# The final output stage in pairs of token tiles: seven block products per pair in place of eight

## What is computed

```python
y = _branch_out(hm.astype(x.dtype), g, w_out)      # (o * silu(g)) @ w_out, 1024 x 1024
return x + gate * y, sf, sb
...
y_sample = _rmsnorm(x, final_norm_w)               # and the same for y_prompt
```

## Time and profile before

| what | value |
|---|---|
| median of the runs | 2621.69 us |
| the profiled execution's own time | 2623.37 us |
| its span, first to last instruction | 2621.6 us |
| TensorE busy | 2573.6 us, 98% of the span |
| VectorE, ScalarE, GpSimd busy | 46%, 34%, 24% |
| mean granted TensorE clock | 0.995 of full speed |

### The profile page before, as it was taken

One profiled execution on the slowest core, in us unless ns is written; L12 is line 12 of the kernel. 1 busy time (PEld: TensorE's weight loads), 2 busy tenths in 40 slices (PEclk: granted clock), 3 DMA queues, 4 the chain that ended last, 5 costly groups with the idle time before them and its releaser, 6 DMA issues.

```text
span 2621.6 us, 49672 instructions
## 1 busy us (share of the span) xinstructions
PE 2573.6 (98%) x18563; PEld 2247.6 (86%) x18563; DVE 1199.6 (46%) x3271; ACT 895.3 (34%) x2118; POOL 623.4 (24%) x816
## 2 busy tenths in 40 slices
PE   6999999999999999999999999999999999999998
PEld 3788888888888887887999999999999999999786
DVE  5664646646465566553242333414242332515433
ACT  5463635626354473223122221313122131314111
POOL 1412232131222213331031120404022130403332
PEclk8999999999999999999999999999999999999999
DMA  9702122030221225431041221304132121316543
GB/s 358 258 23 70 50 58 71 18 98 14 67 64 45 71 63 178 136 122 58 23 75 48 46 85 27 96 17 87 44 59 64 39 85 19 85 44 171 162 146 107
DMA packets 188733, 219.63 MB, mean 84 GB/s; under 512 B 27248, under 2 KB 133504, under 8 KB 186576
## 3 DMA queue, kind: packets, MB, share of 16 engines
q1 hardware_dynamic: 181888, 195.93, 26.8%
q10 hardware_dynamic: 6608, 20.55, 2.0%
HBM read 178.27 MB, written 38.17 MB: 83 GB/s over the span
## 4 chain that ended last, share of the span: by engine, by line
PE 59%; DVE 2%; issue 1%; POOL 0%; ACT 0%; DVEq 0%; POOLq 0%
PE psum L560 12%; PE psum L562 12%; PE psum L561 12%; PE psum L2559 2%; PE psum L2084 2%; PE psum L2626 2%; PE psum L2085 2%; PE psum L2086 2%; PE psum L1611 2%; PE psum L1613 2%; PE psum L1612 2%; PE psum L2629 2%; PE psum L2607 1%; PE psum L2550 1%; PE psum L2514 1%
## 5 line engine op out<-in xcount | busy, mean ns | idle before, releaser
L560 PE MATMUL psum<-h_hi,m_w_lo 128*128 128x384 f32 (+1 forms) x1600 | 594.0, 371 | 0.0
L562 PE MATMUL psum<-h_hi,m_w_hi 128*128 128x384 f32 (+1 forms) x1600 | 573.6, 358 | 0.0
L561 PE MATMUL psum<-h_lo,m_w_hi 128*128 128x384 f32 (+1 forms) x1600 | 573.1, 358 | 0.0
L562 PEld LDWEIGHTS psum<-h_hi,m_w_hi 128*128 128x128 f32 x1600 | 300.5, 188 | 27.0
L560 PEld LDWEIGHTS psum<-h_hi,m_w_lo 128*128 128x128 f32 x1600 | 301.3, 188 | 24.5 <-issue 1.6
L561 PEld LDWEIGHTS psum<-h_lo,m_w_hi 128*128 128x128 f32 x1600 | 301.6, 189 | 22.4
L560 PE MATMUL psum<-h_hi,attn_w_lo 128*128 128x384 f32 (+1 forms) x800 | 294.1, 368 | 0.6 <-DVE attn_w_lo L545 0.6
L562 PE MATMUL psum<-h_hi,attn_w_hi 128*128 128x384 f32 (+1 forms) x800 | 285.9, 357 | 0.0
L561 PE MATMUL psum<-h_lo,attn_w_hi 128*128 128x384 f32 (+1 forms) x800 | 285.5, 357 | 0.0
L1049 DVE CUSTOM_DVE_ANT_0 arena<-psum,wmask,stats 128x640 f32<-128x640 f32 (+2 forms) x256 | 206.0, 839 | 74.5 <-PE psum L1269 73.7
L963 ACT ACTIVATE arena<-arena,stats 128x640 f32<-128x640 f32 (+2 forms) x272 | 213.5, 786 | 70.9 <-DVE stats L1049 69.9
(11 more groups left out here) (343 smaller groups left out, 4629.4 us busy)
## 6 DMA issues: line engine op xcount, KB each, us to landing
m_bc<-gate_rows_mlstm SPq DMA_DIRECT2D x124, 256.0 KB, 3.4
m_w_raw<-in_mlstm_w_in SPq DMA_DIRECT2D x40, 512.0 KB, 4.8
h_full<-gated_output SPq DMA_DIRECT2D x29, 512.0 KB, 4.2
gated_output<-gT SPq DMA_DIRECT2D x8, 1088.0 KB, 5.2
layer_output<-xb_out ACTq DMA_DIRECT2D x17, 512.0 KB, 2.6
h_hi_full<-layer_output SPq DMA_DIRECT2D x17, 512.0 KB, 4.9
out<-h_hi_full ACTq DMA_DIRECT2D x17, 512.0 KB, 5.2
attn_w_raw<-in_attn_w_in SPq DMA_DIRECT2D x16, 512.0 KB, 6.5
```

The source lines that it names most:

```text
L560: pe.matmul(out, self.lo[:, k, :], E.h_hi[:, k, tok], start=(k == 0), stop=False)
L561: pe.matmul(out, self.hi[:, k, :], E.h_lo[:, k, tok], start=False, stop=False)
L562: ins = pe.matmul(out, self.hi[:, k, :], E.h_hi[:, k, tok], start=False, stop=(k == KT - 1))
```

## The change

Tiles 0 to 4 stay as they are. Tiles 5 to 16 are taken as six pairs q = 0 to 5, with tiles b = 5 + 2q and a = 6 + 2q. A pair is regarded as a 2 x 2 block matrix: two tiles of tokens by two halves of the contraction. The output weights are a 2 x 2 block matrix too: two halves of the contraction by two halves of the columns. The eight block products of the ordinary scheme become seven products of sums of blocks, each of 12 matmuls of 128x512. What it adds:

- SP: at the head of `sp_late`, four loads of 1 MB with blocks of the output weights and the two 512 KB loads of pair 0; only behind them the `og` load of tile 3. Pairs 1 to 5 are loaded as pairs.
- VectorE: four combinations of weight blocks, 2048 columns wide (`combined`), behind `og_low(3)` and ahead of the gate multiplication of tile 1; four low parts of the same width behind tiles 1 and 2 (`combined_low`); per pair four low parts (`pair_low`, one of 512 and three of 1024 columns), five additions of 512 columns out of PSUM, and two gate multiplications that now read SBUF.
- ScalarE: four high parts of 2048 columns, behind the square of tile 0 and ahead of the square of tile 1; per pair four high parts and two copies out of PSUM (`p1`, `c11`).
- GpSimd: per pair four additions or subtractions of 512 columns per partition (`pair_sums`) in place of two casts.
- TensorE: waits between the seven products of a pair, since three PSUM banks are accumulated into, read in between, and accumulated into again.

Unchanged parts of the helpers, and their allocation, are left out of this cut of the diff:

```diff
+    FIRST = 5
+    PAIRS = (NT - FIRST) // 2
+    ROWS2, ROWS1, S12, S34 = range(4)
...
+    def sp_blocks(self, sp):
+        w_out = self.E.a["mlstm_w_out"][0].rearrange("(k p) m -> p k m", p=P)
+        for i, (k0, c0) in enumerate(((0, 0), (0, 512), (4, 512), (4, 0))):
+            sp.dma_start(self.t_raw[i], w_out[:, k0:k0 + 4, c0:c0 + 512]).then_inc(self.s_tx, 16)
...
+    def pair_sums(self, pool, q):
+        two, one, s12, s34 = self.pair_raw[q % 2]
+        first, second = slice(0, 4), slice(4, 8)
+        a11, a12, a21, a22 = one[:, first, :], one[:, second, :], two[:, first, :], two[:, second, :]
+        s1, s2, s3, s4 = s12[:, first, :], s12[:, second, :], s34[:, first, :], s34[:, second, :]
+        pool.wait_ge(self.s_pair[q % 2], 32 * (q // 2 + 1))
+        if q < 2:
+            pool.wait_ge(self.s_y, (3, self.FIRST)[q])
+        settle(self.E, pool)
+        pool.tensor_tensor(s1, a21, a22, ALU.add).then_inc(self.s_S, 1)
+        pool.tensor_tensor(s3, a11, a21, ALU.subtract).then_inc(self.s_S, 1)
+        pool.wait_ge(self.s_S, 4 * q + 1)
+        pool.tensor_tensor(s2, s1, a11, ALU.subtract).then_inc(self.s_S, 1)
+        pool.wait_ge(self.s_S, 4 * q + 3)
+        pool.tensor_tensor(s4, a12, s2, ALU.subtract).then_inc(self.s_S, 1)
...
+    ORDER = (1, 0, 2, 3)
+
+    def pair_high(self, act, q):
+        act.wait_ge(self.s_pair[q % 2], 32 * (q // 2 + 1))
+        if q == 1:
+            act.wait_ge(self.s_y, self.FIRST)
+        for x in self.ORDER:
+            if x == self.S12:
+                act.wait_ge(self.s_S, 4 * q + 4)
+            act.copy(self.pair_hi[q % 2][x], self.pair_parts(self.pair_raw[q % 2][x], x)).then_inc(self.s_phi, 1)
...
+    def pair_low(self, dve, q, i):
+        if q >= self.PAIRS:
+            return
+        x = self.ORDER[i]
+        dve.wait_ge(self.s_phi, 4 * q + i + 1)
+        dve.wait_ge(self.s_S, 4 * q + 4)
+        dve.tensor_tensor(self.pair_parts(self.pair_lo[q % 2][x], x), self.pair_parts(self.pair_raw[q % 2][x], x),
+                          self.pair_hi[q % 2][x], ALU.subtract).then_inc(self.s_plo, 1)
...
     def sp_late(self, sp):
-        for n in range(3, NT):
+        self.sp_blocks(sp)
+        self.load_pair(sp, 0)
+
+        def next_x(n):
+            sp.wait_ge(self.s_xn, n - 2)
+            self.load_x(sp, n)
+
+        for n in range(3, self.FIRST):
             sp.wait_ge(self.s_y, n - 2)
             self.load_og(sp, n, 0, KT)
-            sp.wait_ge(self.s_xn, n - 2)
-            self.load_x(sp, n)
+            next_x(n)
+        next_x(self.FIRST)
+        for q in range(1, self.PAIRS):
+            if q == 1:
+                sp.wait_ge(self.s_y, self.FIRST)
+            else:
+                sp.wait_ge(self.s_pr, 7 * (q - 1))
+            self.load_pair(sp, q)
+            next_x(self.tiles_of(q - 1)[1])
+            next_x(self.tiles_of(q)[0])
+        next_x(NT - 1)
...
+        for n in range(self.FIRST):
+            residual(n)
+            if n + 3 < self.FIRST:
                 self.og_high(pool, n + 3)
+            if n == 2:
+                self.pair_sums(pool, 0)
+        for q in range(self.PAIRS):
+            if q:
+                for n in self.tiles_of(q - 1):
+                    residual(n)
+            if q + 1 < self.PAIRS:
+                self.pair_sums(pool, q + 1)
+        residual(NT - 2)
...
+        for n in range(self.FIRST):
+            squares(n)
+            if n < self.FIRST - 1:
+                store(n)
+            if n == 0:
+                act.wait_ge(self.s_tw, 4)
+                for i in range(4):
+                    act.copy(self.t_hi[i], self.t_raw[i]).then_inc(self.s_thi, 1)
+            if n == 2:
+                self.pair_high(act, 0)
+        for q in range(self.PAIRS):
+            b, a = self.tiles_of(q)
+            bank = self.banks_of(q)[0]
+            if q:
+                squares(b - 2)
+            act.wait_ge(self.s_pr, 7 * q + 1)
+            if q:
+                act.wait_ge(self.s_v, 5 * q - 1)
+            act.copy(self.p1, bank[:, :]).then_inc(self.s_p1, 1)
+            if q:
+                squares(b - 1)
+                store(b - 2)
+            act.wait_ge(self.s_pr, 7 * q + 3)
+            act.wait_ge(self.s_x1, a - 1)
+            act.copy(self.scaled[a % 2][:, 0:512], bank[:, :]).then_inc(self.s_c11, 1)
+            store(b - 1)
+            if q + 1 < self.PAIRS:
+                self.pair_high(act, q + 1)
+        for n in (NT - 2, NT - 1):
+            squares(n)
+            store(n)
...
+        def combined():
+            x0, x1, x2, x3 = self.t_raw
+            dve.wait_ge(self.s_tx, 64)
+            dve.tensor_tensor(x2, x2, x1, ALU.subtract).then_inc(self.s_tw, 1)
+            dve.tensor_tensor(x1, x1, x0, ALU.subtract).then_inc(self.s_tw, 1)
+            dve.wait_ge(self.s_tw, 1)
+            dve.tensor_tensor(x0, x2, x0, ALU.add).then_inc(self.s_tw, 1)
+            dve.wait_ge(self.s_tw, 3)
+            dve.tensor_tensor(x3, x3, x0, ALU.subtract).then_inc(self.s_tw, 1)
+
+        def combined_low(i):
+            dve.wait_ge(self.s_thi, i + 1)
+            dve.tensor_tensor(self.t_lo[i], self.t_raw[i], self.t_hi[i], ALU.subtract).then_inc(self.s_tlo, 1)
+
+        for n in range(self.FIRST):
+            j = n % 2
+            dve.wait_ge(self.s_y, n + 1)
+            if n >= 2:
+                dve.wait_ge(self.s_x1, n - 1)
+            dve.tensor_tensor(halves(self.scaled[j]), E.PS[:, 2 * j:2 * j + 2, :], halves(gate_of(n)),
+                              ALU.mult).then_inc(self.s_t, 1)
+            if n < self.FIRST - 1:
+                normalised(n)
+            if n + 3 < self.FIRST:
                 og_low(n + 3)
+            if n == 0:
+                combined()
+            if n in (1, 2):
+                combined_low(2 * n - 2)
+                combined_low(2 * n - 1)
+            if n == 3:
+                for i in range(4):
+                    self.pair_low(dve, 0, i)
+        for q in range(self.PAIRS):
+            b, a = self.tiles_of(q)
+            last = q == self.PAIRS - 1
+            second, third = self.banks_of(q)[1:]
+            later, sooner = self.scaled[a % 2], self.scaled[b % 2]
+            left, right = slice(0, 512), slice(512, 1024)
+            dve.wait_ge(self.s_pr, 7 * q + 2)
+            dve.wait_ge(self.s_p1, q + 1)
+            dve.tensor_tensor(self.u2, second[:, :], self.p1, ALU.add).then_inc(self.s_v, 1)
+            if q:
+                normalised(b - 2)
+            normalised(b - 1)
+            dve.wait_ge(self.s_pr, 7 * q + 4)
+            dve.tensor_tensor(self.u3, second[:, :], self.p1, ALU.add).then_inc(self.s_v, 1)
+            self.pair_low(dve, q + 1, 0)
+            self.pair_low(dve, q + 1, 1)
+            dve.wait_ge(self.s_pr, 7 * q + 5)
+            dve.wait_ge(self.s_v, 5 * q + 2)
+            dve.wait_ge(self.s_x1, b - 1)
+            dve.tensor_tensor(sooner[:, right], third[:, :], self.u3, ALU.add).then_inc(self.s_v, 1)
+            self.pair_low(dve, q + 1, 2)
+            if last:
+                dve.wait_ge(self.s_c11, q + 1)
+                dve.tensor_tensor(later[:, left], later[:, left], gate_of(a)[:, left], ALU.mult).then_inc(self.s_half, 1)
+                dve.wait_ge(self.s_half, 1)
+                dve.wait_ge(self.s_x[a % 3], 16 * (a // 3 + 1))
+                dve.tensor_tensor(self.xb[a % 3][:, left], self.xb[a % 3][:, left], later[:, left], ALU.add).then_inc(self.s_last, 1)
+            dve.wait_ge(self.s_pr, 7 * q + 6)
+            dve.tensor_tensor(sooner[:, left], second[:, :], self.p1, ALU.add).then_inc(self.s_v, 1)
+            dve.wait_ge(self.s_v, 5 * q + 4)
+            dve.tensor_tensor(sooner, sooner, gate_of(b), ALU.mult).then_inc(self.s_t, 1)
+            self.pair_low(dve, q + 1, 3)
+            dve.wait_ge(self.s_pr, 7 * q + 7)
+            dve.wait_ge(self.s_x1, a - 1)
+            dve.tensor_tensor(later[:, right], third[:, :], self.u2, ALU.add).then_inc(self.s_v, 1)
+            dve.wait_ge(self.s_v, 5 * q + 5)
+            if last:
+                dve.tensor_tensor(later[:, right], later[:, right], gate_of(a)[:, right], ALU.mult).then_inc(self.s_half, 1)
+                dve.wait_ge(self.s_half, 2)
+                settle(E, dve)
+                dve.tensor_tensor(self.xb[a % 3][:, right], self.xb[a % 3][:, right], later[:, right], ALU.add).then_inc(self.s_last, 1)
+            else:
+                dve.wait_ge(self.s_c11, q + 1)
+                dve.tensor_tensor(later, later, gate_of(a), ALU.mult).then_inc(self.s_t, 1)
+        normalised(NT - 2)
+        normalised(NT - 1)
...
-        for n in range(1, NT):
+        for n in range(1, self.FIRST):
...
+        def product(q, out, slot, side, w, start):
+            x = 0 if slot == self.ROWS2 else side
+            hi = self.pair_hi[q % 2][slot][:, x, :, :]
+            lo = self.pair_lo[q % 2][slot][:, 4 * side:4 * side + 4, :]
+            for k in range(4):
```

(74 more changed lines are left out.)

36 lines of the change are left out of this document (34 added, 2 removed).

## The result

The changed kernel took 2639.8 us (median of 4 runs, 2638.31 to 2641.01), beside 2621.73 for the kernel before on the same chip (4 runs, 2621.37 to 2622.23): ratio 1.0069, interval 1.0056 to 1.0081. It is slower by 18 us. The prediction said 2641.5, range 2628 to 2650, slower with 0.87.

What follows compares the result with a forecast made beforehand. TensorE, busy 98% of the span, was taken as the bound. Saving -16.35, start-up +29.3, steady pairs +4 and tail +2.9 gave +19.85 us: 2641.5 from a median of 2621.69, range 2628 to 2650.

Steps and rivals of the forecast that it cites:

- stall ahead of tile 3: Start-up: TensorE waits 9.8 us for tile 1's gate, behind tile 3's late rows and four combinations on VectorE.
- stall ahead of tile 4: Start-up: TensorE waits 5.5 us for tile 2's gate, behind ScalarE's casts and VectorE's low parts.
- product 1 of pair 0: Start-up: TensorE waits 10.5 us for the pair's first low part, including up to 3.0 for turns with GpSimd.
- product 3 of pair 0: Start-up: TensorE waits 3.5 us for ScalarE's copy of the first bank, behind VectorE's low parts and gate 4.
- start-up together: The four stalls, ahead of tiles 3 and 4 and two products of pair 0, add 29.3 us.
- steady pairs: Six pairs: turns between VectorE and GpSimd delay ScalarE's copy and the addition ahead of product 7, 4 us in all.
- tail: Kernel end: tile 16's square waits behind tile 15's store, so the last store goes out 2.9 us later.
- The low bound: Start-up: stalls of 19.0 us if rows and blocks did not delay each other and there were no port turns.
- The clock: After start-up stalls TensorE may run at 0.50; costed at nothing, up to 2.7 us once at pair 0's third product.
- A: Rival, start-up covered: stalls sum to less than 13.4 us, so faster, 2620.4, or 2608.3 fully covered; chance 0.08.
- B: Rival, start-up and pairs: only SP's queue misread, no GpSimd turns; stalls 19.0, total +5.5, 2627.2 us; chance 0.12.
- C: Rival, steady pairs: additions out of PSUM also wait for GpSimd, 12 us in place of 4, 2649.5; chance 0.13.

Runs made afterwards that it cites:

- saving_alone: Kernel before the change, with six of the 48 matmuls of each of tiles 5 to 16 left out and nothing added: 2605.91 us, ratio 0.9934.
- rows_first: Changed kernel with SP loading tile 3's rows ahead of the weight blocks: 2635.75 us, ratio 1.0049 to the kernel before.
- sums_copied: Changed kernel with GpSimd's four sums per pair replaced by ScalarE copies: 2638.97 us, ratio 1.006 to the kernel before.
- both: Changed kernel with tile 3's rows loaded ahead of the blocks and VectorE's and ScalarE's work reordered (gate 1 before combinations): 2623.72 us, ratio 1.0002.

## Why the prediction was right

By its steps, predicted and measured in us (starts from the timelines; a stall is the start less the start that matmuls at 0.227 us would give):

| step | predicted | measured |
|---|---|---|
| 72 matmuls fewer | -16.35 | -17.0 by `saving_alone` |
| stall ahead of tile 3 | 9.8 | 11.95 (2470.38 less 2458.43) |
| stall ahead of tile 4 | 5.5 | 4.9 (15.77 from tile 3's start) |
| product 1 of pair 0 | 10.5 | 9.6 (20.49 from tile 4's start) |
| product 3 of pair 0 | 3.5 | 3.1 (8.58 from product 1's start) |
| start-up together | 29.3 | 29.5 |
| steady pairs | 4 | 2.3 |
| tail | 2.9 | 2.6 (8.34 from the last matmul's end to the store, 5.71 before) |
| stage began earlier | none | -0.6 |

With -16.35 for the saving, the measured terms sum to +17.5; the spans differ by 17.6, and the prediction's sum was 19.85.

*Start-up.* All four waits are where the prediction put them, each for the instruction that it named. Their sum is nearer than the parts deserve: errors of either sign cancel, which is luck. Tile 3 was mis-sized by 2.1 us: the sum gave 2455.9 for the landing, and the cast began at 2457.86. The long issues of SP's queue are not shown to be the reason, since the DMA engines were busy throughout (359 GB/s from 2440 to 2457.5, above). What moved was more than the 5.77 MB that the sum counted: ScalarE issued tile 0's store of 0.52 MB in that time.

```profile
2445.78 0.35 ACTq L2152 DMA_DIRECT2D out<-h_hi_full  x1
```

At 359 GB/s it takes 1.5 us, an estimate that would cover most of the 2 us; no run tries the load without it. The three later terms were 1.9 too high together, by tenths at most steps: tile 1's reciprocal, for one, came 7.5 us after tile 3's start for the 7.9 of the sum, and instructions in a row start 0.08 us before the one ahead ends. The wide operations took what two narrower widths had given, 2.28 to 2.29 us on VectorE for the 2.3 of the sum.

*The low bound.* The prediction's bound from below, 19.0 us of stalls, rested on a stall of 2.5 ahead of tile 3 if its rows and the blocks did not hold each other up. `rows_first` took 4.9 us off, not 7.3: the blocks had landed at 2455.2 and not 2451.1. Tile 3's own load stood ahead of them there, 1.6 us at the prediction's 330 GB/s; the other 2.5 are not taken apart. So the bound was too low for this way of mending the order.

*The clock.* After TensorE had stood idle for 11.69, 3.31 and 7.75 us the granted clock was low. Windows of the changed kernel behind the three stalls (0.50 is 1.2 GHz; the clock stands behind POOL's busy time):

```profile
2470.40:2473.10 2.70, 2.70 (x7) 2.12 (x8) 0.00 (x0) 2.70 (x3) 2.67 (x2) 0.50 0.00 0
...
2486.20:2490.30 4.10, 4.10 (x11) 3.24 (x12) 0.16 (x1) 1.44 (x3) 4.09 (x3) 0.58 0.00 0
...
2506.60:2510.60 4.00, 3.96 (x9) 3.14 (x10) 4.00 (x4) 0.00 (x0) 0.00 (x0) 0.50 0.72 252
```

Seven to eleven matmuls each ran in windows granted 0.50 to 0.58, and tile 3, tile 4 and the first two products took 1.6, 1.9 and 2.2 us longer than at full clock. That is why the idle time that TensorE shows (11.69 + 3.31 + 7.75 + 0.92 = 23.7) is 5.9 less than the 29.5 by which the starts were late: part of each stall is slow work instead of idleness (1.6 + 1.9 + 2.2 = 5.7). The next start was set by VectorE's or ScalarE's list each time, so it cost nothing more, as the prediction had it. The Trainium skill (TensorE: Matmul & The Clock Gate, "HAM oscillation — how this bites in real kernels") tells of a kernel whose matmuls start slow behind every long wait for a DMA, and counts the slow part as added time. This trace agrees on the slow matmuls and not on the added time, since here another engine's chain covers them.

*Steady pairs.* 480 matmuls from 2515.22 on took 2.3 us over their 109.0. The turns between VectorE and GpSimd are there. Source lines of the changed kernel (min/median/max ns): the gate multiplication of the later tile, which meets GpSimd in every pair, that of the earlier tile, and an addition out of PSUM.

```profile
L2289 DVE TENSOR_TENSOR h_full<-h_full,h_hi_full x5: 2701/2705/2706, 2530.2 to 2608.9; 128x1024 f32<-128x1024 f32 x5
```

```profile
L2276 DVE TENSOR_TENSOR h_full<-h_full,h_hi_full x6: 1225/1226/1227, 2527.2 to 2624.5; 128x1024 f32<-128x1024 f32 x6
```

```profile
L2274 DVE TENSOR_TENSOR h_full<-psum,pair_sum x6: 684/686/692, 2526.4 to 2623.8; 128x512 f32<-128x512 f32 x6
```

L2289 takes 2.70 us for its 1.23, as long as it must wait for the running residual. But VectorE has the room. Waits of TensorE's weight loads from 2515.5 to 2627 us:

```profile
PEld psum L2334 <- DVE h_full L2265: 1.7, 3, 0.6
PEld psum L2334 <- ACT pair_sum L2172: 1.3, 4, 0.3
```

The two waits that I had followed through are there, the addition ahead of product 7 and ScalarE's first copy ahead of product 3, but in three and four pairs and not in all, and the copy at 0.3 us for the 0.6 of the sum. The weight loads waited 3.0 us together and the matmuls lost 2.3. So the 4 us were mis-sized by 1.7.

*The rivals.* A (covered) falls: it needed stalls under 13.4 us. B (only SP's queue misread, no turns) falls: tile 3's rows came later than forecast, not earlier, and `sums_copied` shows the turns. C (additions out of PSUM wait for GpSimd too) falls by this pair of rows, the timelines of VectorE and GpSimd during pair 0:

```profile
2529.44 0.68 DVE L2280 TENSOR_TENSOR h_full<-psum,pair_sum 128x512 f32<-128x512 f32 x1
```

```profile
2528.59 3.18 POOL L2089 TENSOR_TENSOR h_hi_full<-h_hi_full,h_full 128x1024 f32<-128x1024 f32 x1 [9.44 <-DVE h_full L2276]
```

The addition ran inside the residual's time and took 0.68 us, as in all six pairs (683 to 692 ns). The Trainium skill (SBUF — State Buffer, "SBUF: two separate sides") says that of VectorE's plain operations only those with two SBUF inputs compete with GpSimd; both halves of that agree with these rows.

## What to carry to other kernels

A saving on the bound engine is worth what its start-up leaves of it: list, for each engine's in-order queue, what stands ahead of the first instruction that the bound engine waits for, and move one-off preparation behind it. Look for the second way round before undoing the first: here the late load held the stage through VectorE's list and, once that was opened, through GpSimd's, so that tile 3's stall went only with both edits. A load that is due soon belongs ahead of bulk loads in its queue (4.9 us here). When you add up what stands ahead of a load, count the traffic of the other queues too.

## What was not expected

- SP's issues can take long: with the four 1 MB loads and one of 512 KB ahead, the second pair load took 6.58 us to issue in the changed kernel (6.77 in `rows_first`, 6.78 in `both`), where the same load takes 0.58 when it comes again for two later pairs. What stands behind is issued late. Since the DMA engines were busy all the while, it is not shown that anything landed later for it, and why the issue takes so long was not tried.
- The low clock after a gap shows in the trace as a shorter wait: 5.7 us of the start-up's delay are matmuls at half speed, and a reading of idle time alone would have put the stalls too low by a fifth.
